# q and k normalised rows transposed back in full fp32 and split into hi and lo on the way out of PSUM, in a fused decoder-layer kernel

## The reference, cut to what matters

```python
xn = rms_norm(h, norm_g)
z = xn @ w_in
u, zp, q, k, v, za, ga, gb = jnp.split(z, IN_SPLIT_POINTS, axis=-1)
q = rope(rms_norm(q.reshape(B, T, N_HEADS, HEAD_DIM), q_norm_g), pos)      # 16 heads of 64
k = rope(rms_norm(k.reshape(B, T, N_KV_HEADS, HEAD_DIM), k_norm_g), pos)   # 4 heads of 64
v = v.reshape(B, T, N_KV_HEADS, HEAD_DIM)
...                                   # sliding-window attention with sinks, both token groups
yb = o.reshape(B, T, ATTN_WIDTH).astype(h.dtype) * jax.nn.silu(za)
m = jax.nn.sigmoid(ga) * (ya @ w_proj_pool) + jax.nn.sigmoid(gb) * (yb @ w_proj_attn)
h = h + m @ w_out
```

## Time and profile before

| | |
|---|---|
| median of 3 runs | 1253.31 us |
| the profiled execution | 1254.71 us |
| its span, first to last instruction | 1252.9 us |
| TensorE matmul busy | 1215.4 us (97%) |
| VectorE busy | 540.8 us (43%) |
| ScalarE busy | 419.1 us (33%) |
| GpSimd busy | 409.6 us (33%) |
| mean granted TensorE clock | 0.99 |

### The profile page before, as it was taken

One profiled execution on the slowest core, in us unless ns is written; L12 is line 12 of the kernel. 1 busy time (PEld: TensorE's weight loads), 2 busy tenths in 40 slices (PEclk: granted clock), 3 DMA queues, 4 the chain that ended last, 5 costly groups with the idle time before them and its releaser, 6 DMA issues.

```text
span 1252.9 us, 19582 instructions
## 1 busy us (share of the span) xinstructions
PE 1215.4 (97%) x7688; PEld 1190.8 (95%) x7688; DVE 540.8 (43%) x906; ACT 419.1 (33%) x886; POOL 409.6 (33%) x189
## 2 busy tenths in 40 slices
PE   4899999899999999999999999999999999999997
PEld 4899889899999999999999999999999999999997
DVE  5869776211244444444433615481042151064321
ACT  4233333334267777777740101130020020041111
POOL 2333223223312222221144533424325335254410
PEclk8899999999999999999999999999999999999999
DMA  7313425531243434333351111116232233231211
GB/s 288 115 57 115 169 104 155 162 100 51 72 127 120 133 105 136 118 95 108 110 190 50 58 53 44 36 38 242 86 97 91 85 107 125 77 102 64 73 36 52
DMA packets 135948, 129.82 MB, mean 104 GB/s; under 512 B 40319, under 2 KB 123415, under 8 KB 135887
## 3 DMA queue, kind: packets, MB, share of 16 engines
q1 hardware_dynamic: 118487, 102.25, 26.6%
q10 hardware_dynamic: 17400, 26.71, 5.8%
HBM read 93.25 MB, written 37.71 MB: 105 GB/s over the span
## 4 chain that ended last, share of the span: by engine, by line
PE 88%; DVE 9%; DMA 1%; issue 1%; ACT 0%; SPq 0%; ACTq 0%; DVEq 0%
PE ps L576 75%; PE ps L770 4%; PE ps L748 2%; PE ps L758 2%; DVE sa L993 1%; DVE xn L938 1%; DVE sa L979 1%; DVE m_lo L942 1%; DVE sa L989 1%; DVE stack L973 1%; DVE hs L981 1%; DVE stack L971 1%; PE ps L631 1%; PE ps L603 1%; PE ps L687 1%
## 5 line engine op out<-in xcount | busy, mean ns | idle before, releaser
L576 PE MATMUL ps<-m_hi,w_hi 128*128 128x352 f32 x2016 | 664.5, 331 | 8.3 <-DVE m_lo L942 8.3
L576 PE MATMUL ps<-m_lo,w_hi 128*128 128x352 f32 x2016 | 650.0, 323 | 0.0
L576 PE MATMUL ps<-m_hi,w_lo 128*128 128x352 f32 x2016 | 435.9, 324 | 0.0
L576 PEld LDWEIGHTS ps<-m_hi,w_hi 128*128 128x128 f32 x2016 | 381.0, 189 | 12.6 <-issue 6.9
L576 PEld LDWEIGHTS ps<-m_lo,w_hi 128*128 128x128 f32 x2016 | 380.9, 189 | 1.0 <-issue 1.0
L576 PEld LDWEIGHTS ps<-m_hi,w_lo 128*128 128x128 f32 x2016 | 345.5, 189 | 0.0
L511 POOL TENSOR_TENSOR w_hi<-raw_a,w_one 128x1024 fp32r<-128x1024 f32 x42 | 80.9, 1926 | 778.4 <-PE ps L576 527.1
L513 POOL TENSOR_TENSOR w_lo<-raw_b,w_hi 128x1024 fp32r<-128x1024 f32 x42 | 111.4, 2652 | 3.3
L513 POOL TENSOR_TENSOR w_lo<-raw_a,w_hi 128x1024 fp32r<-128x1024 f32 x42 | 109.6, 2609 | 3.3
L511 POOL TENSOR_TENSOR w_hi<-raw_b,w_one 128x1024 fp32r<-128x1024 f32 x42 | 89.9, 2141 | 0.0
L1070 DVE TENSOR_TENSOR pt_lo<-ps,pt_hi 128x512 fp32r<-128x512 f32 x64 | 41.2, 686 | 58.5 <-ACT pt_hi L1402 58.5
(11 more groups left out here) (183 smaller groups left out, 1158.3 us busy)
## 6 DMA issues: line engine op xcount, KB each, us to landing
raw_a<-in_w_in SPq DMA_DIRECT2D x26, 512.0 KB, 3.7
raw_b<-in_w_in SPq DMA_DIRECT2D x26, 512.0 KB, 4.0
qk_d<-qkst ACTq DMA_DIRECT2D x10, 1056.0 KB, 4.3
gate_d<-gst ACTq DMA_DIRECT2D x16, 528.0 KB, 4.3
gin<-gate_d SPq DMA_DIRECT2D x16, 528.0 KB, 3.6
qt<-qk_d SPq DMA_DIRECT2D x32, 256.0 KB, 3.2
xT_d<-sa SPq DMA_DIRECT2D x4, 1056.0 KB, 7.4
yb_d<-sa SPq DMA_DIRECT2D x1, 4224.0 KB, 12.9
```

The source lines that it names most:

```text
L576: last = nc.tensor.matmul(ps[:, 3 * parity + c, 0:CH], w, x[:, k, CH * c:CH * c + CH], start=(k == 0 and w is wh and x is src_hi), stop=(k ...
```

## The change

Four things, all in the q, k, v projection.

- The rows stay unsplit for q and k. TensorE transposes the row buffer itself, full fp32: three back rounds a tile (4, 4 and 1 transposes) and not five. Both heads of a tile lie on the partitions together. ScalarE copies a round to the high part of `qkst`, VectorE subtracts that from the same PSUM bank for the low part (`low_parts`). `qkst` has two buffers.
- Three row buffers in place of two. `stack` has one buffer and is used for v alone.
- The squares move from VectorE to ScalarE (`square`).
- The store of a tile (`store_qk`) is two DMAs of 64 partitions and stands at the start of a later tile's list. A bank is free again when ScalarE (rows) or VectorE (back) says so.

The diff, cut to its core:

```diff
-            qkst = sb("qkst", [P, 2, T], F32R, scope=s1)
-            stack = sb("stack", [P, 2, (PBLK + 1) * 256], F32R, scope=s1)
+            qkst = sb("qkst", [P, 2, 2, T], F32R, scope=s1)
+            stack = sb("stack", [P, (PBLK + 1) * 256], F32R, scope=s1)
...
@@ TensorE, turn()
-                        ge(pe, stack_done, j + 1)
-                    src = st32[:, j % 2, :].rearrange("p (b h e) -> p b h e", h=2, e=P)
-                    for b in range(4 if i < 4 else 0):
-                        last = nc.tensor.transpose(ps[:, bank, P * b:P * b + P], src[:, 4 * (i % 2) + b, i // 2, :], ident)
-                    for b in range(2 if i == 4 else 0):
...
+                        pe.wait_ge(rope_done, j + 1)
+                    src = rows[:, j % 3, :]
+                    for b in range(4 if i < 2 else 0):
+                        c0 = P * (4 * i + b)
+                        last = nc.tensor.transpose(ps[:, bank, P * b:P * b + P], src[:, c0:c0 + P], ident)
+                    if i == 2:
+                        last = nc.tensor.transpose(ps[:, bank, 0:NS], src[0:NS, SEQ:SEQ + P], ident[0:NS, 0:NS])
...
@@ VectorE
+            def low_parts(j):
+                for i in range(3):
+                    bank = 6 + BACK_ROUND[j][i] % 2
+                    c0, w = 512 * i, (512 if i < 2 else NS)
+                    dve.wait_ge(back_hi, 3 * j + i + 1)
+                    v.tensor_tensor(qkst[:, j % 2, 1, c0:c0 + w], ps[:, bank, 0:w], qkst32[:, j % 2, 0, c0:c0 + w],
+                                    ALU.subtract).then_inc(back_free, 1)
             for j in range(12):
...
+                if j == 2:
+                    low_parts(0)
+                if 2 <= j < 11:
+                    low_parts(j - 1)
                 if j < 10:
-                    step.did(v.tensor_tensor(sq, x, x, ALU.mult))
-                    step.settle()
+                    dve.wait_ge(sq_done, j + 1)
...
@@ ScalarE
+            def square(j):
+                act.wait_ge(rows_free, 3 * j + 3)
+                ge(act, hms_done, j)
+                a.activation(sq_rows, rows[:, j % 3, :], ACT.Square).then_inc(sq_done, 1)
+            def store_qk(j):
+                act.wait_ge(back_free, 3 * j + 3)
+                for h in range(2):
+                    act.dma_start(qk_d[2 * j + h].rearrange("(s e) n -> e s n", s=2),
+                                  qkst32[HD * h:HD * h + HD, j % 2]).then_inc(qk_stored[j % 2], 16)
...
@@ plan_rounds(), tiles from 3 on
-            rows(j - 1, 2 if j == 7 else 1)
...
-                back(j - 2 if j >= 7 else j - 3, j - 1 if 5 <= j <= 10 else None, 5 if j == 7 else 4)
+            if j - 2 < 10:
+                here.append((0, "std", j - 2, 0, 0))
+            if 4 <= j:
+                here.append((0, "store", j - 3, 0, 0))
+            rows(j - 1, 1)
             if j == 3:
+                back(0, (4, 4, 5))
+                back(1, (6, 6, 7), store_in=0)
+            elif j < 12:
+                back(j - 2, (5, 6, 7))
```

More of the change, by code:

```diff
@@ L316, in build @@
         state_rows = kv_out[:].rearrange("p a n -> p (a n)")
-        rows = saf[:, 2880:2880 + 2 * (PBLK + 1) * P].rearrange("p (s n) -> p s n", s=2)
+        rows = saf[:, 2880:2880 + 3 * (PBLK + 1) * P].rearrange("p (s n) -> p s n", s=3)
+        sq_rows = saf[:, 1056:1056 + (PBLK + 1) * P]
+        qkst32 = qkst[:].bitcast(F32)
         m_hi32, m_lo32 = m_hi[:].bitcast(F32), m_lo[:].bitcast(F32)
@@ L371, in _ @@
             for tiles, a, b in ((8, 0, NH), (10, NH, NH + NKV)):
-                sp.wait_ge(qk_stored, 16 * tiles)
+                for h in range(2):
+                    sp.wait_ge(qk_stored[h], 16 * tiles)
                 for half in range(2):
@@ L657, in rounds @@
                 for step, kind, jj, i, r in plan:
-                    if kind == "std":
+                    if kind not in ("rows", "back"):
                         continue
@@ L996, in _ @@
                     v.tensor_tensor(x1, tmp[0], tmp[1], ALU.subtract)
-                    step.did(v.tensor_tensor(x2, tmp[2], tmp[3], ALU.add))
-                    step.settle()
-                if j >= 8:
+                    v.tensor_tensor(x2, tmp[2], tmp[3], ALU.add).then_inc(rope_done, 1)
+                    if j >= 8:
+                        dve.wait_ge(rope_done, j + 1)
+                        keep_kv(j)
+                else:
+                    dve.wait_ge(rows_free, 3 * j + 3)
                     keep_kv(j)
-                split_rows(j)
+                    split_rows(j)
             dve.wait_ge(q_loaded, 16 * 8)
@@ L1337, in _ @@
                         head_std(jj)
+                    elif kind == "square":
+                        square(jj)
+                    elif kind == "store":
+                        store_qk(jj)
                     else:
@@ L1586, in rows, with back @@
             here.append((at + i, "rows", j, i, r))
+            freed.append(("rows", 3 * j + i + 1))
             r += 1
-        rows_end[j] = r
-    def back(j, std=None, at=4):
+        if j < 10:
+            here.append((0, "square", j, 0, 0))
+    def back(j, at, store_in=None):
         nonlocal r
-        for i in range(5):
-            if i == 2 and std is not None:
-                here.append((0, "std", std, 0, 0))
-            here.append((at + i * 3 // 5, "back", j, i, r))
+        for i in range(3):
+            if i == 2 and store_in is not None:
+                here.append((0, "store", store_in, 0, 0))
+            here.append((at[i], "back", j, i, r))
+            back_round.setdefault(j, []).append(r)
+            freed.append(("back", 3 * j + i + 1))
             r += 1
-        back_end[j] = r
     for j in range(2, 13):
```

81 lines of the change are left out of this document (32 added, 49 removed).

## The result

The changed kernel took 1261.79 us (median of 6 runs, 1255.44 to 1262.45) beside 1253.8 us for the kernel before on the same chip (6 runs): a ratio of 1.0054, 95% interval 1.0038 to 1.007. It is 8.0 us slower, against a forecast of +8.6. A second set of six runs gave 1261.51 us and 1.0058. The profiled execution was 1255.44 us, the fastest of its six; where its own parts differ from the median's, the text says so.

A forecast was written before the change was run, and what follows sets the result against it. TensorE, busy 97% of the span, was taken as the bound. -18.1 (work and old waits) + 14.4 (four waits) + 12.3 (end) = +8.6 us on 1253.31 gave 1262 us, 8-in-10 range 1250 to 1270.

The forecast's parts named there:

- TensorE's work: Back transposes, 0.99 us less a tile; with the old waits gone the projection would end 18.1 us earlier.
- Four waits: Tiles 4, 6, 8, 10: TensorE idle 2.3 to 3.0 us from E (tile's end) + 9.9, awaiting VectorE's GpSimd-held chain.
- The clock behind them: Low granted clock behind each of the four waits; wait and clock together 3.6 us each, 14.4 us in all.
- The end: Behind tile 11's end (E): late stores and loads put the sample scores at E + 25.6, not 15.0; +12.3 us.
- The wait at the small rows: TensorE waits 2 to 4 us at the small rows round behind tile 11, released by ScalarE, costing nothing more.
- The wait at the scores: TensorE idle about 9 us at the sample scores behind the projection.
- the chain fits: Rival: VectorE gets its turns quickly, TensorE hardly waits in tiles 4 to 10; -10 us, 1243 us; 13%.
- the end is covered: Rival: `stack_done` early and stores landing fast, the end costs 3 to 5 us, four waits stay; 1253.6 us; 12%.
- the third: Rival: every wait drops the clock and the halves of the stores are slow; +18 us, 1271 us; 7%.

The follow-up runs named there:

- the kernel in which GpSimd is late: Changed kernel with GpSimd beginning a pair of weight chunks only when the next tile's rotation is through: 1245.74 us, ratio 0.9928.
- VectorE's order: Changed kernel with tile 10's values split ahead of tile 9's low parts on VectorE alone: 1255.62 us, ratio 1.0018.
- both orders: Changed kernel with tile 10 split ahead of tile 9's low parts and tile 9's store issued ahead of v's: 1252.94 us, ratio 0.9983.
- the whole store: Changed kernel with `qk_d` laid out so that a tile's store is one transfer of 128 partitions, not two halves: 1260.47 us, ratio 1.0051.
- the repeat: The changed kernel run once more, unaltered, with a second profile: 1261.51 us, ratio 1.0058.

## Why the prediction was right

The forecast of 1262 came out, and so did its mechanism. That the median (1261.79) lies so near it is partly luck: the terms as measured below sum to 5.8 us in the first profile and 6.9 in the second, against 8.6 forecast and 8.0 and 6.9 between the medians. Term by term:

- **TensorE's work, -18.1.** Right. The period without waits was 13.82 us where 13.77 was worked out. Eight tiles at 13.82 would be 110.6 us, 17.8 less than before.
- **Four waits.** Right in number, place and cause; the kernel in which GpSimd is late shows all three. The length was 2.2 us where 2.3 to 3.0 was given. The chain ended 12.04 us behind GpSimd's start against 11.97 taken over from the earlier trace rows; TensorE reached its wait 9.98 us behind GpSimd's start (97.62), some 0.3 later than reckoned (E + 9.9, with GpSimd's start at about E + 0.25); 0.1 of that is a slip, as 8.4 + 1.45 + 0.12 is 9.97.
- **The clock behind them, 3.6 each.** Too much. The two prices are real (2.4 and 3.9 us), but the high one was paid once in four in the first profile and twice in the second. Four cost 121.8 - 110.6 = 11.2 us and 123.4 - 110.6 = 12.8, not 14.4. What decides stays open: of the equal waits in tiles 4, 6, 8 and 10, the clock fell behind tile 6's in both profiles and behind tile 10's in the second alone. It isn't the tile: in the five profiles with these waits of 2.21 us (the changed kernel twice, VectorE's order, both orders, the whole store) it fell behind 9 of 20, in tiles 4, 6, 8 and 10 alike, and never behind two in a row. Taking the middle of the two prices for all four, on one row at either, was a guess, and 1.6 to 3.2 us too high in all (the middle of 2.3 and 4.7 is 3.5, too, and not 3.6).
- **The end, +12.3.** Measured 12.4, and 11.9 in the repeat. The sum was right, but by errors that cancel, which is luck: `stack_done` came 2.4 us earlier than reckoned, SyncE began 3.0 later behind it, and its loads took 1.0 less. `stack_done` came at E + 6.1 and not 8.5: the copies met GpSimd, but the cast did not (0.74 us), and only the subtraction did (3.44). Then the stores: SyncE began 10.5 us behind `stack_done`, where I had 7.5 and a bound of 9.9. Both were made with the landing of the old, whole store. With a whole store behind v's (the layout experiment) SyncE began 229.78 - 221.59 = 8.2 us behind v's issue, inside the bound and 0.7 above the 7.5; with the halves 226.14 - 215.67 = 10.5. So the two halves cost 2.3 us there, and they are what put it 0.6 outside the bound. SyncE's loads took 4.7 us and not 5.7, the rest was as worked out: E + 25.2 against 25.6.
- **The wait at the small rows.** 2.7 us, inside 2 to 4, and covered by the later one as said. The wait at the scores was 7.5 and 8.4 us, against about 9.

The first two rivals (the chain fits, the end is covered) are refuted by the waits: four of 2.2 us, and 7.5 at the scores. Of the third, the halves of the stores are slower than the whole, and the clock is lost behind some waits only.

The Trainium skill (SBUF — State Buffer, "Who interferes with whom") was drawn on for which VectorE instructions GpSimd can hold. The traces agree: the subtraction out of PSUM is 0.69 us beside GpSimd's work (at 102.73 in the kernel in which GpSimd waits for the chain) as without it, the sum over heads 1.34 and 1.35, while L1005, with two inputs in SBUF, goes from 1.36 to 3.25 and the four of L1009 from 0.97 to 4.71. The same page (section "Door 1: The DMA port swizzle") let me estimate that two halves of 64 partitions would land 2.4 us later than one whole. The runs gave 6.0 against 4.1 us, 1.9 later, and 2.3 later behind v's store. The sign and most of the size are right, and it is the part that my own bound had left out; I had kept the estimate beside the sum and not in it.

## What to carry to other kernels

A chain of small instructions on VectorE cost here what it met: look at which other engine is released by the same event as the chain, and let the one with slack wait for the other. When work is taken off the bounding engine, ask of every consumer that moved behind a later producer how much time is left to the place where it is wanted; here 9.5 us were left (88.10 to 97.62) for a chain of 5.95, and 11.6 were needed. In a list worked through in order, one late store made all that stood behind it late, so what is wanted first is issued first (8.6 us here).

## What the hardware did that I had not expected

- With stores whose outermost dimension in HBM has two entries, the core moved 52 GB/s at a DMA share of 0.13, and two issues held the issuing engine for 17 us.
- The same idle time of 2.21 us of TensorE was followed by the granted clock of 1.00 or by a stretch at 0.62, in one execution.
- Start-up differs: the place behind tile 1 lies between 58.59 and 64.62 us over the thirteen profiles, though the work ahead of it is nearly the same. In the first pair that was 5.1 us, as much as most of the change's effect, and a reason to compare stretches and medians, not the ends of one pair.
